# A two-layer hybrid trunk on one core: order of the weight loads, their place before the count of rounds, and four edits around the router

## The reference, cut to what matters

```
h = rmsnorm(x, mix_norm[layer])
x = x + (even_mixer if layer == 0 else odd_mixer)(h, ...)
h = rmsnorm(x, ffn_norm[layer])
x = x + hier_moe(h, wg, bg, we, be, w1, w3, w2)

def hier_moe(h, ...):
    gprob = softmax(t @ wg + bg);  gval, gidx = top_k(gprob, 1)        # one of 4 groups
    elog  = (t @ we + be) of that group;  ev, ei = top_k(softmax(elog), 2)
    gate  = gval * ev / sum(ev), spread over 32 experts
    for e in range(32):
        y += gate[:, e] * ((silu(t @ w1[e]) * (t @ w3[e])) @ w2[e])
```

## Time and profile before

| | kernel before |
|---|---|
| median of 3 runs | 1291.18 us |
| the profiled execution | span 1289.3 us from its first to its last instruction; the page gives no other time for it |
| TensorE matmul (PE) | 1132.1 us busy, 88%, 9125 instructions |
| TensorE weight load (PEld) | 639.1 us, 50% |
| VectorE (DVE), ScalarE (ACT), GpSimd (POOL) | 359.7 us (28%), 216.9 us (17%), 18.3 us (1%) |
| moved by DMA | 458.90 MB, mean 356 GB/s |
| the chain that ended last | PE 49%, DMA 23%, SP's queue 14%, DVE 4% |
| mean granted TensorE clock | 0.980 |

### The profile page before, as it was taken

One profiled execution on the slowest core, in us unless ns is written; L12 is line 12 of the kernel. 1 busy time (PEld: TensorE's weight loads), 2 busy tenths in 40 slices (PEclk: granted clock), 3 DMA queues, 4 the chain that ended last, 5 costly groups with the idle time before them and its releaser, 6 DMA issues.

```text
span 1289.3 us, 21411 instructions
## 1 busy us (share of the span) xinstructions
PE 1132.1 (88%) x9125; PEld 639.1 (50%) x9125; DVE 359.7 (28%) x989; ACT 216.9 (17%) x435; POOL 18.3 (1%) x20
## 2 busy tenths in 40 slices
PE   7999989999887787787999999989999887878777
PEld 5667454554443434243788875454554443434332
DVE  4795341111111101112747553241111110101111
ACT  1315130010000000001324552030110010000000
POOL 0121000000000000000000000000000000000000
PEclk9999999999999999989999999999999998999998
DMA  9920599999999999999944446579999999999996
GB/s 385 381 76 1 216 420 429 427 429 426 429 429 427 429 430 426 429 429 426 383 164 164 170 157 258 198 278 429 427 427 428 430 429 427 430 429 427 429 428 282
DMA packets 33935, 458.90 MB, mean 356 GB/s; under 512 B 3776, under 2 KB 3936, under 8 KB 6240
## 3 DMA queue, kind: packets, MB, share of 16 engines
q1 hardware_dynamic: 32688, 454.00, 84.0%
q10 hardware_dynamic: 1200, 4.23, 0.9%
HBM read 457.13 MB, written 1.08 MB: 355 GB/s over the span
## 4 chain that ended last, share of the span: by engine, by line
PE 49%; DMA 23%; SPq 14%; DVE 4%; issue 2%; ACT 1%; another core or an unknown queue 0%; DVEq 0%
DMA ring<-in_moe_units 15%; SPq L346 13%; PE bank L750 10%; PE bank L690 9%; PE bank L660 9%; DMA extra<-in_moe_units 8%; PE bank L680 5%; PE bank L852 4%; PE bank L638 3%; PE bank L588 2%; PE bank L650 1%; PE bank L421 1%; PE bank L809 1%; PE bank L554 1%; PE bank L612 1%
## 5 line engine op out<-in xcount | busy, mean ns | idle before, releaser
L690 PE MATMUL bank<-hT,pgT 128*128 128x512 f32 x512 | 241.6, 615 | 0.0
L660 PE MATMUL bank<-ring,xT 128*32 128x256 f32 x2560 | 166.7, 402 | 45.2 <-DMA ring<-in_moe_units 44.8
L690 PEld LDWEIGHTS bank<-hT,pgT 128*128 128x128 f32 x512 | 94.4, 195 | 134.9 <-issue 117.9
L660 PEld LDWEIGHTS bank<-ring,xT 128*32 128x32 f32 x2560 | 81.7, 111 | 125.9 <-DMA ring<-in_moe_units 68.3
L750 PE MATMUL bank<-h,ring 128*128 128x256 f32 x576 | 130.1, 382 | 0.0
L1492 DVE TENSOR_TENSOR hT<-hT,bank 128x128 f32<-128x128 f32 x64 | 18.4, 287 | 393.8 <-ACT hT L1015 393.8
L660 PE MATMUL bank<-extra,xT 128*32 128x256 f32 x1536 | 101.5, 408 | 27.9 <-DMA extra<-in_moe_units 27.9
L750 PEld LDWEIGHTS bank<-h,ring 128*128 128x128 f32 x576 | 107.4, 190 | 16.5 <-issue 3.0
L660 PEld LDWEIGHTS bank<-extra,xT 128*32 128x32 f32 x1536 | 52.5, 112 | 84.0 <-DMA extra<-in_moe_units 45.5
L1021 ACT ACTIVATE hT<-bank 128x512 f32<-128x512 f32 x64 | 38.2, 597 | 305.0 <-PE bank L680 305.0
L680 PE MATMUL bank<-extra,hT 128*32 128x512 f32 x512 | 66.9, 642 | 20.9 <-DMA extra<-in_moe_units 11.4
(11 more groups left out here) (295 smaller groups left out, 929.5 us busy)
## 6 DMA issues: line engine op xcount, KB each, us to landing
ring<-in_moe_units SPq DMA_DIRECT2D x112, 2048.0 KB, 47.5
extra<-in_moe_units SPq DMA_DIRECT2D x80, 2048.0 KB, 48.1
ring<-in_od_in_units SPq DMA_DIRECT2D x10, 2048.0 KB, 36.9
ring<-in_ev_in_units SPq DMA_DIRECT2D x5, 2048.0 KB, 28.2
ring<-in_od_out_units SPq DMA_DIRECT2D x4, 2048.0 KB, 7.9
ring<-in_ev_out_units SPq DMA_DIRECT2D x2, 2048.0 KB, 23.4
hT<-sums ACTq DMA_DIRECT2D x4, 512.0 KB, 4.3
every<-sums ACTq DMA_DIRECT2D x4, 512.0 KB, 6.1
```

The lines of the kernel that those rows point to most:

```text
L660: last = mm(bank[4 + e % 2][32 * j:32 * j + 32, 0:256], xT[:, 4 * part + k, CAP * e:CAP * e + CAP], w[:, k, :, 256 * (j // 2) + j % 2:256 ...
L690: last = mm(bank[2 * t + h][:, :], pgT[:, e, t, :], ys[:, 512 * h:512 * h + 512], start=False, stop=closed)
```

## The change

Six edits, in both layers. (1) `FIRST` becomes one list for each layer. In layer 0 the units (2, 0) and (2, 1), which go to ring slots, stand ahead of the three of expert 1, and (3, 1) ahead of (2, 2). In layer 1 only (3, 1) moves ahead of (2, 2). (2) The 12 loads of the second step are written out ahead of SyncE's wait for `rt_ok`, and its loop begins at 1. (3) In layer 0 the router's product goes to bank 4 (layer 1 has it there already), and all four `keep_x` stand directly behind it; the wait for `lg_ok` is gone, and `fold` is raised before the rank products. (4) In step 0 `up(0, 1)` stands before `gates` instead of behind it. (5) ScalarE applies Silu to one column of `ones` behind the exponential. (6) VectorE reads the router's product from bank 4 in both layers.

```diff
-FIRST = [(0, 0), (0, 1), (0, 2), (1, 0), (1, 1), (1, 2), (2, 0), (2, 1), (2, 2), (3, 0), (3, 1), (3, 2)]
+FIRST = ([(0, 0), (0, 1), (0, 2), (2, 0), (2, 1), (1, 0), (1, 1), (1, 2), (3, 1), (2, 2), (3, 0), (3, 2)],
+         [(0, 0), (0, 1), (0, 2), (1, 0), (1, 1), (1, 2), (2, 0), (2, 1), (3, 1), (2, 2), (3, 0), (3, 2)])
...
-                for e, part in FIRST:
+                for e, part in FIRST[layer]:
...
+                for e, part in ORDER:
+                    sp.wait_ge(used[layer], finished(e, part))
+                    moe_unit(layer, e, part, GROUP + e)
                 sp.wait_ge(rt_ok, layer + 1)
...
-                with sp.Fori(0, last_step) as i:
+                with sp.Fori(1, last_step) as i:
...
-                        last = mm(bank[4 * layer][:, 36 * t:36 * t + 36], hT[:, k, P * t:P * t + P], wr[:, layer, k, :], start=(k == 0), stop=(k == KT - 1))
+                        last = mm(bank[4][:, 36 * t:36 * t + 36], hT[:, k, P * t:P * t + P], wr[:, layer, k, :], start=(k == 0), stop=(k == KT - 1))
...
-                for a in (1, 2, 3):
-                    keep_x(a)
+                for a in range(4):
+                    last = keep_x(a)
+                last.then_inc(fold, 1)
...
-                pe.wait_ge(lg_ok, 2 * layer + 2)
-                keep_x(0).then_inc(fold, 1)
...
                         gather(1, (2, 3))
+                        pe.wait_ge(m["xt_ok"], i * 2 + 2)
+                        up(0, 1)
                         gates(0); gates(1)
...
-                    pe.wait_ge(m["xt_ok"], i * 2 + 2)
-                    up(0, 1)
+                        pe.wait_ge(m["xt_ok"], i * 2 + 2)
+                        up(0, 1)
...
                 fn(arg[:, :, :], arg[:, :, :], ACT.Exp).then_inc(rt_ex, 1)
+                fn(st[:, 62:63], ones[:, 0:1], ACT.Silu)
...
-                    stt(lg[:, t, :], bank[4 * layer][:, 36 * t:36 * t + 36], st[:, 8 + t:9 + t], br[:, layer, :], ALU.mult, ALU.add).then_inc(lg_ok, 1)
+                    stt(lg[:, t, :], bank[4][:, 36 * t:36 * t + 36], st[:, 8 + t:9 + t], br[:, layer, :], ALU.mult, ALU.add).then_inc(lg_ok, 1)
```

## The result

The changed kernel takes 1284.49 us (median of 4 runs, 1281.37 to 1286.55) against 1291.23 (median of 4, 1291.11 to 1293.34). The ratio is 0.9941, with a 95% interval from 0.9928 to 0.9954, 6.7 us by the medians and 7.6 by the ratio, whose interval is 5.9 to 9.3 us. The forecast was 1281.1, a gain of 10.1 us: the direction was right, and a quarter to a third of the gain is missing. The profiled execution is the slowest of the four, with a span of 1284.8 us.

What follows compares the result with a forecast made beforehand. The prediction took each MoE part to be bound by a transfer row that never pauses, so only its head could be shortened: 5.2 us in layer 0 plus 4.9 in layer 1, 10.1 off 1291.2, gives 1281.1 (8 in 10: 1278.8 to 1285.6).

Steps and rivals of the forecast that it cites:

- What bounds the kernel, and that it passes through: Both MoE parts: unpausing transfer rows at 427 GB/s, 4.9 us a unit; 10.1 us gained at the heads reaches the end.
- signs of being wrong: DMA pauses behind step 1's third load, no wait for the last unit at both ends, or clock falling in layer 1's mixer.
- The two moved loads: Layer 0: (2, 0), (2, 1) go into idle DMA time; seven units remain behind 143.29, six landing by 175.4.
- `fold`: Layer 0: step 0's last load is issued at 176.2 instead of 178.2 and lands at 183.8 instead of 191.5.
- the count: SyncE's read after step 1's 12 loads is hidden, loads being issued some 9 us ahead of their turn.
- One reading: Profile slices: between the two MoE parts lie stretches in which almost nothing is moved.
- The issue times at full clock: Layer 0 loads issued at 176.2, 182.75, 186.7 and 192.9; layer 1 at 857.5, 861.4 and 867.6, less the shift.
- The term that was mis-sized: Landing of step 1's third load, (0, 2), in layer 0: 7.6 to 8.6 us after issue, 200.5 to 201.5, was 206.5.
- The second reckoning, by bytes: At 4.9 us a unit, (0, 2) gains only 4.3 us in layer 0 and 3.9 in layer 1.
- Rival B: New heads: queue runs dry more often, each restart costs 1 us more; 3.3 us a layer, 1284.6; chance 0.18.
- estimate of 6.8 us for a lone load: From the skill page, 2.0 us fixed plus bytes at 436 GB/s; (0, 2) 0.8 us earlier a layer, sum 11.7.
- Silu and `up(0, 1)`: Step 0: (0, 1) issued at 186.7 instead of 189.87, gates 0.6 us later; Silu 0.7 earlier, its table loaded while ScalarE idles.

Runs made afterwards that it cites:

- x_loads: The kernel before with SyncE's edits alone (both new FIRST lists, step 1's loads ahead of the count); TensorE and ScalarE as before: 1283.95 us, ratio 0.9948.
- x_count: The kernel before with one edit, the second step's 12 loads ahead of the read of the count: 1287.93 us, ratio 0.9968.
- x_tensor: The changed kernel with SyncE's queue as in the kernel before: 1291.79 us, ratio 0.9997.
- x_tail: The changed kernel with 4 added matmuls before waits for weight units of experts 1 to 3 in each layer's last step: 1284.09 us, ratio 0.9938.
- x_fold_back: The changed kernel with the copy of x into bank 0, and with it fold, behind the rank products again: 1285.09 us, ratio 0.9942.
- x_act_queue: The changed kernel, but ScalarE's queue issues the last load of step 0 (into extra3): 1283.97 us, ratio 0.9932.
- x_warm: The changed kernel with 11 added matmuls, results unused, in TensorE's waits at the transposes of x, the gates and the first turn: 1284.77 us, ratio 0.9941.
- x_swap: The changed kernel with up(1, 0) of step 0 ahead of the first turn and down, and step 1's early loads in that order: 1283.04 us, ratio 0.9930.
- x_nosilu: The changed kernel without the early Silu line: 1286.93 us, ratio 0.9966.
- x_held: The changed kernel, but SyncE issues (0, 0) of step 1 only when (0, 1) is free too: 1290.34 us, ratio 0.9989.
- x_up_back: The changed kernel with up(0, 1) behind the gates again in step 0: 1284.89 us, ratio 0.9952.

## Why the prediction was right or wrong

*What bounds the kernel, and that it passes through:* right. In every kernel the landing of step 1's fourth load, (1, 0), fixed the end of layer 0: it moved from 211.3 to 208.3, 208.0, 211.0 and 212.5 us in the changed kernel, x_loads, x_count and x_tensor (by -3.0, -3.4, -0.3 and +1.2), and the last product of the layer from 604.50 by -3.2, -3.5, -0.2 and +1.1. From the landing of step 1's fourth load to that of the layer's last unit it took 393.0 to 393.3 us, in both layers of all 14 profiles. The prediction's signs of being wrong didn't come: no pause in the rows, TensorE's wait for the last unit at both ends (1.12 and 1.11 us), full clock in layer 1's mixer.

*The two moved loads, `fold`, the count:* right in the main. In layer 0 the early loads alone give 0.2 to 0.3 us, with the new order 3.4. Seven units behind 143.29 leave the DMA dry before the last one is issued (61 GB/s at 174 to 176 us), though the sixth of them landed at 176.5 and not by 175.4: it was issued with one load in flight, 4.1 us before that one landed, and came 6.0 us behind it. The fold's place in the order moved nothing that arrives at (0, 2). The read of the count was hidden: the 393 us hold with it in either place. One reading was off: the slices between the two MoE parts show 157 to 278 GB/s, and only slices 3 and 4, ahead of the first, are nearly empty.

*The issue times at full clock:* right. Forecast 176.2, 182.75, 186.7 and 192.9, in x_tail 176.0, 182.5, 186.4 and 192.3. In layer 1 of the changed kernel, with the 1.5 us added by which that layer's start had shifted, they were 857.4, 861.4 and 867.2, against 857.5, 861.4 and 867.6. The landings of (0, 0) and (0, 1) in x_tail fit too: 190.4 to 191.4 and 4.9 behind it were forecast, 191.3 and 196.0 came.

*The term that was mis-sized:* "With 7.6 to 8.6 us to land: 200.5 to 201.5". The row went from issue to landing in 10.0, and (0, 2) landed at 202.3. I had taken the end of a lone load from rows with an empty queue and the end of a queued one from rows with a deep one, and a load issued 3.8 us before its only predecessor lands is neither. Layer 0 gains 206.5 - 202.3 = 4.2 us, not 5.2. In layer 1 (0, 2) was issued at 865.7 and landed 10.5 later, 876.2, 6.4 behind (0, 1); that layer gains 3.3, not 4.9. Together 7.5 us, near the ratio's 7.6; as the interval is 5.9 to 9.3 and the two layers come from two profiles, that near a match is partly luck, but the forecast's 10.1 lies outside. In x_loads and x_fold_back about the same time was lost at (0, 0) instead (10.3 and 9.7 us from issue to landing, forecast 7.6 to 8.6), so the mis-sized term is the price of a restart, wherever in the head it falls. The second reckoning, by bytes, had come out at 4.3 and 3.9, much nearer, and I had called it a bound. That is luck: it kept the landing at 200.5, which was wrong, and made up for it by taking 1.7 us from the old row. Rival B had this mechanism, a restart dearer by 1 us, and priced it at 3.3 us a layer and 1284.6, within 0.2 of the median: its chance of 0.18 was too low. The other way, the prediction's estimate of 6.8 us for a lone load, is not borne out: 156 loads issued with none in flight took 7.5 to 9.3 us, half of them 7.7 or less.

*Silu and `up(0, 1)`:* they are a pair, which the forecast did not say. With both undone (x_loads, where the fold and the bank are undone too) the gain is 6.7 us, with one undone 4.4 (no Silu) or 6.2 (`up` back), with both 7.6. Moving `up` ahead puts the gates 0.6 us later, and then the table load stands bare behind them; before, `up(0, 1)` had covered it. How much the pair adds over x_loads, 0.9 us by the ratios, lies within their intervals.

*The clock:* whether the stretch at half clock in the head is tied to the edits is open. In the profiles it began at 171.7 to 172.6 us in the changed kernel (twice), x_tensor, x_warm, x_swap and x_nosilu, and not in the kernel before, x_count, x_loads, x_act_queue, x_tail, x_fold_back, x_held and x_up_back. The changed kernel and x_tail are the same up to the last step and stand on either side, so chance has a part. Of the 11 profiles with the edits of TensorE and ScalarE 6 had it, of the 3 without them none, which is too few to tell. In x_act_queue and x_held a stretch began at 190.9 and 190.6 instead. With the stretches at 172.2 and 192.6 (the first profile) (0, 2) was issued 2.6 us later and landed 1.1 later than at full clock (x_tail). Why it comes in some executions only stays open. It and the first end (7.16 or 8.79 us from the last unit to the mixer) may make up a good part of the spread between runs (1281.4 to 1286.6 us for the changed kernel). As only one run of each kernel has a trace, that is not shown.

## What to carry to other kernels

Where a row of large loads never pauses, only its head can be shortened; follow one load behind which the row is full, from its issue to its landing, in both kernels. Price a load by the queue depth it meets and by how early it is issued: here 7.5 to 9.3 us for 2 MB alone, 4.9 behind the one before in a deep row, but some 10 from issue with one other in flight that lands 4 us later. When an edit moves work ahead of other work, ask what the moved piece had been covering: here a table load.

## What the runs showed of the hardware

How far a load lands behind the only other one in flight went with how early it was issued. In the 14 profiles 26 loads were issued 3.6 to 4.3 us before the other landed: all came 5.8 to 7.3 us behind it. Of the 63 issued 4.8 us or more before, 61 came 4.7 to 5.1 us behind, as in a full row. Of the six issued 3.0 to 3.6 us before, the distances go from 4.9 to 6.9. In x_tail (0, 2) was issued 3.8 us before and came 6.2 behind; (0, 1) was issued 4.9 before and came 4.7 behind. The rate fell with it from 427 to 303 GB/s for 2 us while the DMA engines counted as busy. Why is open; a second issuing queue did not help. A distance of 6 us is no proof of a shallow queue by itself: the ninth load of step 0 in the kernel before, issued at 150.4 us with five in flight, landed 6.3 us behind its predecessor, with 426 GB/s or more at 170 to 178 us.

TensorE fell to half clock for some 3 us in the midst of work, in some executions and not in others. Four added wide matmuls shortly ahead did not keep it up. With seven more behind, the next such stretch was gone, but it was gone in x_swap too, which had none, so that the matmuls did it is not shown.
